# A fused decoder layer: filler products on TensorE and a new order of work in its opening

## What is computed

```python
h = rms_norm(x, norm1_g[l])                     # y = x * rsqrt(mean(x*x) + EPS) * g
qa, ka, va, qb, kb, vb, gb, gate_a, gate_b = jnp.split(h @ w_in[l], split_idx, axis=-1)
qa = apply_rope(rms_norm(qa...), positions, ROPE_DIM, ROPE_THETA)   # needs sin and cos of positions
```

## Time and profile before

| | |
|---|---|
| median of 3 runs | 1431.59 us (1431.24 to 1432.26) |
| the profiled execution, its own time | 1431.52 us |
| its span, first to last instruction | 1429.8 us |
| PE busy | 1403.3 us, 98% of the span |
| DVE busy | 1077.9 us, 75% |
| ACT busy | 848.3 us, 59% |
| POOL busy | 408.6 us, 29% |

### The profile page before, as it was taken

The page is one execution under the profiler, slowest core; times in us unless marked ns, Lnnn a source line. Parts: engine busy times, 40 slices in busy tenths (PEclk is TensorE's granted clock), DMA queues, the critical chain, the costliest instruction groups (busy, mean ns, idle before and its releaser), DMA issues.

```text
span 1429.8 us, 19786 instructions
## 1 busy us (share of the span) xinstructions
PE 1403.3 (98%) x7265; PEld 1187.3 (83%) x7266; DVE 1077.9 (75%) x1570; ACT 848.3 (59%) x1399; POOL 408.6 (29%) x463
## 2 busy tenths in 40 slices
PE   7999999999999999999999999999999999999997
PEld 6888988988988888888888888888888888888885
DVE  7855764664674797666832669999999999999996
ACT  5643453453354363353332248888888888888883
POOL 3325424424433400000000122333333333333331
PEclk9999999999999999999999999999999999999999
DMA  5210110210210143343432469999999999999991
GB/s 176 63 45 18 46 45 1 64 45 2 63 32 23 48 105 97 102 145 90 127 133 87 179 222 420 401 390 386 389 386 393 393 390 393 389 399 404 396 408 46
DMA packets 129236, 283.86 MB, mean 199 GB/s; under 512 B 18281, under 2 KB 93169, under 8 KB 104562
## 3 DMA queue, kind: packets, MB, share of 16 engines
q1 hardware_dynamic: 115584, 261.48, 49.4%
q0 software_dynamic: 13248, 21.00, 4.0%
q10 hardware_dynamic: 306, 0.07, 0.0%
HBM read 284.60 MB, written 25.17 MB: 217 GB/s over the span
## 4 chain that ended last, share of the span: by engine, by line
PE 96%; DVE 1%; ACT 1%; DMA 0%; issue 0%; POOL 0%; POOLq 0%; ACTq 0%; DVEq 0%
PE proj L178 18%; PE proj L180 18%; PE proj L179 18%; PE scores L180 7%; PE scores L178 7%; PE scores L179 7%; PE scores L830 2%; PE outs L907 2%; PE scores L687 2%; PE turned L178 1%; PE turned L180 1%; PE turned L179 1%; PE turned L687 1%; PE outs L1017 1%; PE turned L870 1%; PE outs L180 1%
## 5 line engine op out<-in xcount | busy, mean ns | idle before, releaser
L2139 DVE TENSOR_TENSOR w_low<-w_slot,w_high 128x2048 fp32r<-128x2048 f32 x192 | 430.8, 2285 | 0.1
L1427 ACT ACTIVATE w_high<-w_slot 128x2048 fp32r<-128x2048 f32 x190 | 349.5, 1905 | 3.0 <-DMA w_slot<-in_w_up 3.0
L178 PE MATMUL proj<-w_high,xeH 128*128 128x512 f32 x512 | 202.1, 395 | 0.3 <-DVE xeL L2245 0.3
L180 PE MATMUL proj<-w_high,xeL 128*128 128x512 f32 x512 | 200.0, 391 | 0.0
L179 PE MATMUL proj<-w_low,xeH 128*128 128x512 f32 x512 | 199.6, 390 | 0.0
L1636 POOL DMA_INDIRECT out<-y,ids_rows x31 | 86.6, 2793 | 338.2 <-DVE y L2261 338.2
L180 PEld LDWEIGHTS proj<-w_high,xeL 128*128 128x128 f32 x512 | 96.1, 188 | 20.1
L178 PEld LDWEIGHTS proj<-w_high,xeH 128*128 128x128 f32 x512 | 96.6, 189 | 19.4 <-issue 0.4
L179 PEld LDWEIGHTS proj<-w_low,xeH 128*128 128x128 f32 x512 | 96.3, 188 | 19.1
L178 PE MATMUL proj<-wBH,hTH 128*128 128x512 f32 x256 | 111.9, 437 | 0.0
L178 PE MATMUL proj<-wAH,hTH 128*128 128x384 f32 x256 | 99.2, 388 | 2.0 <-DVE wAL L1695 2.0
(11 more groups left out here) (468 smaller groups left out, 3297.5 us busy)
## 6 DMA issues: line engine op xcount, KB each, us to landing
w_slot<-in_w_gate SPq DMA_DIRECT2D x64, 1024.0 KB, 7.5
w_slot<-in_w_up SPq DMA_DIRECT2D x64, 1024.0 KB, 7.5
w_slot<-in_w_down SPq DMA_DIRECT2D x64, 1024.0 KB, 7.6
gate_raw<-in_w_in SPq DMA_DIRECT2D x56, 256.0 KB, 2.9
wB_in<-in_w_in SPq DMA_DIRECT2D x16, 512.0 KB, 5.9
wA_in<-in_w_in SPq DMA_DIRECT2D x9, 512.0 KB, 6.1
wC_in<-in_w_branch_a SPq DMA_DIRECT2D x16, 256.0 KB, 2.8
wC_in<-in_w_branch_b SPq DMA_DIRECT2D x16, 256.0 KB, 3.2
```

Source lines behind the costliest of these rows:

```text
L178: pe.matmul(out, lh, rh, start=start, stop=False, skip_group_check=onto)
L180: return pe.matmul(out, ll, rh, start=False, stop=stop, skip_group_check=onto)
L1427: act.activation(w_high[slot][:], w_in6[slot][:], ACT.Copy).then_inc(S["w_split"], 1)
L2139: dve.tensor_tensor(w_low[slot][:], w_in6[slot][:], w_high[slot][:].bitcast(F32), ALU.subtract).then_inc(S["w_lows"], 1)
```

## The change

Four engines are touched, all in the opening.

- PE: six small products of ones with ones (128 columns, float32) before the positions are turned, eight products of the identity with itself before tile 0 is turned, and six more behind that. They write a PSUM bank whose content is not used. `ones_made` is a new semaphore for the column of ones, so the counts on `g1_in` go down by one.
- ACT: tile 0 is squared before both copies of the norm row. The first four weight pieces are rounded in a row. Then come the square of tile 1, sine and cosine, and the last four pieces.
- POOL: the power for tile 0 alone comes first, then the two small gain operations, then the power for tile 1, then the wait for sine and cosine.
- DVE: the last angle step (L1910) moves from before `low_tile(0)` to after the second low piece of the weights. Mean and scaling of tile 1 move one piece up.

```diff
 # PE
+            def stay_awake(n, one, many):
+                for _ in range(n):
+                    pe.matmul(bank(3)[:, 0:128], one, many, start=True, stop=True)
+
+            pe.wait_ge(S["ones_made"], 1)
+            stay_awake(6, ones_row[:], ones_row[:])
             pe.wait_ge(S["ang_step"], 1)
             pe.transpose(TB[:, 0:8], pos_rows_f[:], ident[0:8, 0:8]).then_inc(S["first_turned"], 1)
-            pe.wait_ge(S["g1_in"], DMA + 1)
+            pe.wait_ge(S["g1_in"], DMA)
             for half, spare in enumerate((PROJ[1], OB)):
                 pe.matmul(spare[:, :], ones_row[:], g1_one[:, half * 512:half * 512 + 512], start=True, stop=True
                           ).then_inc(S["first_turned"], 1)
+            stay_awake(8, ident, ident)
             turn_tile(0)
+            stay_awake(6, ident, ident)
 # ACT
+            square_tile(0)
             for half, spare in enumerate((PROJ[1], OB)):
-                if half == 1:
-                    square_tile(0)
                 act.wait_ge(S["first_turned"], 2 + half)
                 act.activation(g1_row[:, half * 512:half * 512 + 512], spare[:, :], ACT.Copy).then_inc(S["g1_in"], 1)
             high_tile(0)
             for k in range(8):
-                if k == 2:
+                if k == 4:
+                    square_tile(1)
                     act.wait_ge(S["ang_step"], 9)
                     act.activation(sin_t[:], ang[:], ACT.Sin).then_inc(S["trig_done"], 1)
                     act.activation(cos_t[:], turns[:], ACT.Sin, scale=-1.0, bias=const("half_pi")).then_inc(S["trig_done"], 1)
-                if k == 4:
-                    square_tile(1)
                 high(wAH[:, k, :], wA_in[:, k, :], S["wA_first" if k < 4 else "wA_landed"], 3 * DMA, S["wA_high"])
 # POOL
-            pool.memset(ones_row[:], 1.0).then_inc(S["g1_in"], 1)
+            pool.memset(ones_row[:], 1.0).then_inc(S["ones_made"], 1)
...
-            x_powers(range(2))
-            pool.wait_ge(S["trig_done"], 3)
+            x_powers([0])
             pool.wait_ge(S["gains_in"], 2 * DMA)
             pool.tensor_scalar(gains[:, 0, :], gains[:, 0, :], 0.125, None, ALU.mult).then_inc(S["tables_made"], 1)
             pool.wait_ge(S["tables_made"], 3)
             pool.tensor_scalar(rope_sin[:, 0:2, 0, :], gains[:, :, 8:16], -1.0, None, ALU.mult).then_inc(S["tables_made"], 1)
             pool.wait_ge(S["tables_made"], 4)
+            x_powers([1])
+            pool.wait_ge(S["trig_done"], 3)
 # DVE
-                    dve.wait_ge(S["g1_in"], DMA + 3)
+                    dve.wait_ge(S["g1_in"], DMA + 2)
...
-            angle(dve.scalar_tensor_tensor(turns[:], ang[:], -1.0, ang[:], ALU.mult, ALU.max))
             low_tile(0)
             for k in range(8):
+                if k == 2:
+                    angle(dve.scalar_tensor_tensor(turns[:], ang[:], -1.0, ang[:], ALU.mult, ALU.max))
+                if k == 3:
+                    mean_tile(1)
                 if k == 4:
-                    mean_tile(1)
-                if k == 5:
                     norm_tile(1)
                 low(wAL[:, k, :], wA_in[:, k, :], wAH[:, k, :], S["wA_high"], k + 1, S["wA_low"])
```

More of the change, by code:

```diff
@@ L472, in decoder_layer @@
             oTA qkS_done vg_done tanh_done cosB sinB ropedB sg_done qkTB kv_done U_done
-            st_done sT_done oB bn_step bn_r onR_done gate_step gated gTB gate_sums h_step h_high h_low
+            st_done sT_done oB bn_step bn_r onR_done gate_step gated gTB gate_sums h_step h_high h_low ones_made
             wC_high wC_low oT_high oT_low c_done gate_out sig_mul merged_step
```

## The result

The changed kernel takes **1434.32 us** (median of 22 runs, 1432.62 to 1435.34) against 1431.86 (22 runs, 1430.10 to 1432.52): ratio 1.0016, 95% interval 1.0010 to 1.0023. It is 2.5 us slower where 0.6 us faster was forecast. It lies outside the range (1429.3 to 1433.4) and inside the 0.2% that count as no change. The profiled execution took 1434.82 us, with a span of 1433.0.

A forecast was written before the change was run, and what follows sets the result against it. From 12.64 us DVE was taken to have least air in the opening. Tile 2 0.35 us sooner plus a vanished 0.33 us wait made 0.7, taken as 0.6 off 1431.52: 1430.9 us, range 1429.3 to 1433.4.

The forecast's parts named there:

- The six of ones: Fillers ahead of the positions: 2.65 us at the low level, ending at 6.25, first angle step 2.2 us late.
- The eight of identity: Fillers ahead of tile 0, from 10.1 us: at the high level 1.8 us, done at 11.9, hidden behind the tile's wait.
- the slower rival: Opening: level stays low, eight fillers delay tile 0, tile 2 scaled at 25.8; 1.5 us slower, 1433.0; chance 0.20.
- Transposes at 12.05: PE in the opening: tile 0 ready to be turned at 12.05 us, 1.34 later than before.
- The low estimate: Eight fillers ahead of tile 0 at the low level: 3.5 us, ending at 13.6 and delaying tile 0 by 1.55.
- DVE to tile 2: Low part of tile 0 to scaling of tile 2: 10.25 us instead of 11.36, tile 2 at 23.65, 0.35 sooner.
- The end moves by what the opening moves: Whole kernel: PE's work behind the opening is fixed, so what the opening loses is not won back.
- PE's lead passed on: Opening: PE, not DVE, was the bound, so its 2.3 us lead at tile 0's projection reaches the end; 1429.2; chance 0.13.
- The gain being eaten: From 12 us on: DVE's sum of work counts, later start and extra step cancel saved waits; 1431.6 within 0.5; chance 0.15.

The follow-up runs named there:

- e3: Kernel before with five identity products added among the gate products near 650 us, opening untouched: 1432.32 us against 1431.80.
- e9: Changed kernel with every product ahead of tile 0 on 128 rows, identity replacing ones and norm row (computes another layer): 1432.03 us against 1431.36 before.
- e4: Changed kernel with the late block of identity products before the first expert cut from 20 to 10: 1433.03 us against 1431.80 before.
- e10: Changed kernel without its 20 fillers, but four identity products ahead of tile 0 and four behind it: 1431.05 us against 1431.36 before.
- e1: Kernel before with the 20 opening fillers added, old order on ACT, POOL and DVE kept: 1433.93 us against 1431.80.
- e12: e10 with the late block of identity products before the first expert cut from 20 to 16: 1430.35 us against 1431.36 before.

## Why the prediction was wrong

- **The six of ones: right.** The first angle step came at 6.54 (6.65 forecast), the norm row's products ended at 10.0 (10.1), and the scaling of tile 0 was at 10.74 (10.7), bounded by the copy of the norm row.
- **The eight of identity: wrong, and this step decided.** The prediction put them at the high level, "By then PE has worked 6.5 us without a gap, more than the 3.8 us that did nothing". They ran low for all their 3.58 us. I counted the length of the work and not its kind: 6.4 of the 6.5 us were products of one row, and the only such work in the profile of before, 4.15 to 7.91 us, had left the pace low. The other leg, the 3.7 us after which the pace rose, was one draw: in e3, with the same opening, the pace was up at 17.65, before that stretch began. With 128 rows instead, in e9, the pace was up in time. The prediction names the evidence of the one-row products beside the slower rival and gives that a chance of 0.20.
- **Transposes at 12.05: 13.52.** The low estimate in the same part had 13.6. Behind this step tile 2 was scaled at 25.70 instead of 23.65, and the last turn came 1.1 us later than before where the forecast had 0.6 sooner: 1.7 of the 3.1 us by which forecast and median differ. With the level that the forecast assumed, in e9, the transposes came at 12.13 and tile 2 at 24.10, still 0.45 late, but the last turn was 0.5 us ahead of before, near the forecast.
- **DVE to tile 2: right.** 10.25 us were forecast from the low part of tile 0 to the scaling of tile 2; it took 25.70 - 15.31 = 10.39. But the 11.36 us of before were one draw as well: in e3, with the old order and the pace up at 17.65, the same stretch took 23.34 - 12.63 = 10.71. So 0.65 of the saving was not the order's. The waits for ACT in between are gone, as the chain shows, which runs along DVE from 15.3 to 25.7 us but for two powers on POOL.
- **The slower rival: right for the opening.** It said tile 2 at 25.8, measured 25.70. It said 1.5 us at the end, and the profiles give 1.1.
- **Not in the prediction at all: the late stretch.** "The end moves by what the opening moves" was wrong for the profiled executions, in which the late stretch moved it too. The clock's fall near 836 us was there to be seen, in the windows of the kernel before, and the fillers at 841 us too. The sum left both out. Together they account for 2.2 of the 3.3 us between the profiled executions. Between the medians it is about 1.3, by e4, whose interval overlaps that of the changed kernel. How much of it the change caused, and how much is the draw of the two profiles, is not shown.
- **PE's lead passed on: wrong**, as e10 shows. The gain being eaten: not tested apart from that.

The order was worth more than I gave it: by itself 1.9 us (0.3 to 2.9 by its interval), against the 0.6 forecast for the whole.

What stays open: what sets the moments at which the clock falls and rises near 840 us, and whether a shift of 1 to 3 us makes the long low stretch more frequent. The profiles show what it costs when it comes.

## What to carry to other kernels

A filler is safe only if it ends before the real work is ready at the *low* pace; sized at the high one it grows just when it is needed (here from 4.71 to 7.58 us), and it stands in front of whatever its engine has to do next. Too short is not safe either: the block of 12 ended 2.65 us early, and the clock fell again. Before counting on a filler, look for the same kind of product in the trace and see whether the pace rose behind it. And what is lost early in a kernel may not be the whole difference at its end, where a clock can fall in between: read those places, with the blocks that were sized for them, as part of the sum.

## What the runs showed of the hardware

- Products with one row of weights left the pace low for as long as they ran. In the changed kernel PE worked from 3.46 to 9.94 us on little else, and the next 3.6 us were still low (about 3 in e1 and e4, which start the same way). With 128 rows in their place, and other values, the pace was up by the second wide product, near 7 us.
- The unchanged opening varies by more than a microsecond from run to run. In e3, whose opening is that of the kernel before, the transposes of tile 1 took 1.09 us instead of 1.97 at the same start:

```profile
19.48 1.09 PE L726 MATMUL scores<-consts,x_all 128*128 128x128 f32 x8 [1.10 <-DVE x_all L1870]
```

  Its last turn was at 58.0 instead of 59.2. A profile shows one draw of this. Against that draw the changed kernel's opening is 2.3 us late, not 1.1, and by its other draw, in e4, 1.9.
- The granted clock column says 1.00 over the first 20 us in every profile here, whatever the pace was. Near 838 us the same column says 0.50, and the pace agrees: 40 records in 7.39 us there, 4.71 at 1.00. The Trainium skill (TensorE: Matmul & The Clock Gate, Part 1: The HAM clock gate) advises to cross-check such events; by these numbers the column can be trusted for a fall and the rise behind it, and not before the first of them.
- Tile 0 of x did not always land when I had put it (5.3 us), and this is a draw too. In the ten profiles of the new order its square waited for the transfer, and started between 5.07 (e10) and 7.12 (e12); in the changed kernel's it was 6.42.
